# Reordering the on-chip tensors of an encoder layer so that the large ones begin at multiples of 2048 bytes

## The chip, the cores and the metric

The kernel runs on one core of a Trainium2 chip. The metric is the device time of one execution in microseconds, lower being better. The kernel before takes 1151.82 us, the median of 3 runs (1151.05 to 1152.61).

## The reference, cut to what matters

One layer of a streaming encoder on 256 tokens of width 2048, all in float32:

```python
h   = rms_norm(x, ln1);  p = h @ w_in            # 2048 x 5376
r   = retention(...)     # 8 heads of 128, rotary, group norm, swish gate
s   = sliding_window_attention(...)   # 16 query heads, 2 key/value heads, sinks
x   = x + concat([r, s]) @ w_out                 # 2048 x 2048
u   = rms_norm(x, ln2) @ w_ffn_in                # 2048 x 11264
a,b = split(u);  a = causal_depthwise_conv(a)    # width 3
x   = x + (gelu(a) * b) @ w_ffn_out              # 5632 x 2048
y   = rms_norm(x, ln_f)
```

The weights are about 200 MB and each is read once.

## The kernel before, in words

**Tiles.** Every weight is streamed from device memory in tiles of 128 rows (partitions) by 1024 float32 numbers, 4096 bytes in each partition. SyncE issues the loads into a ring of eight slots, `raw` (lines 313 to 320). ScalarE rounds a tile into `w_hi` (line 720), VectorE writes the difference `raw - w_hi` into `w_lo` (line 957); both are rings of four slots. TensorE multiplies in its one-pass float32 format (float32r) and so needs the activations split in the same way: `h_both` holds the high and low halves of the normalised input side by side, `mix_hi` and `mix_lo` those of the attention's output, `g_hi` and `g_lo` those of the gated hidden layer.

**Two forms of product.** In the input projection, the attention's output projection and the down projection (`three_pass`, lines 413 to 416) a block of activations of 128 columns is the stationary operand and 512 columns of `w_hi` or `w_lo` (256 in the first four tiles, which hold keys and values) are the moving one: `hi*hi`, `hi*lo`, `lo*hi`, three matmuls for each block. In the up projection (`up_tile`, lines 622 to 632) the weights are the stationary operand, four column blocks of 512 bytes each for each row block, and the activations are the moving one. One matmul takes all 512 numbers of a row block of `h_both` (line 630: high and low half at once), the next the 256 of the high half (line 632).

**Order.** The stages run one behind the other: keys and values, queries, eight heads with the attention of one head interleaved between the projection tiles of the next, the output projection, eleven groups of the up projection, the down projection in two sweeps, the last norm. All waits are written out by hand on semaphores: a load waits until its slot in `raw` has been read, ScalarE waits for the load and for the matmuls of the tile four before, VectorE for ScalarE, and TensorE for VectorE.

**Where tensors lie.** On-chip memory is given out in the order of the declarations, each tensor at the next address in the partition that is a multiple of 32 bytes. The first one declared begins at byte 16512 of the partition, which is 8 x 2048 + 128. Declared are first `x_res` (16384 bytes), `raw` (32768), `w_hi` and `w_lo` (16384 each), all of them multiples of 2048 bytes long, so that all four begin 128 bytes past a multiple of 2048. Then come the small ones: `ident` (512 bytes), `cols` (896), `sumsq` (32) and six tensors of 8 bytes, each of which takes 32. The tensors of the first part follow, `h_both`, `mix_hi`, `mix_lo`, `rows` and `rope` at 1760 bytes past a multiple of 2048; behind `mask` (1280 bytes) they lie at various remainders. The second part takes the same space again, with `y_tok`, `lnf_row`, `under_h`, `g_tok`, `g_hi`, `g_lo`, `sums` and `conv`, all of them at remainder 1760.

The slices that the matmuls read are multiples of 512 bytes from the start of these tensors. A moving operand of 512 columns of `w_hi` so begins at remainder 128, one of `h_both` at 1760. In the key and value tiles a row block of weights is 1024 bytes wide and begins at remainder 128 or at 1152, by turns; one that begins at 1152 ends at 2176 and runs over a multiple of 2048, one that begins at 128 does not.

Of the kernel before, what the change touches and what calls it, by code (L numbers as in the profile page):

```python
# [23 lines left out]
F32R = mybir.dt.float32r  # L24
# [6 lines left out]
P = 128  # L31
D_MODEL = 2048
SEQ = 256
TOK = SEQ // P
KT = D_MODEL // P
COLS = 512
# [24 lines left out]
RAW = 8  # L61
SPLIT = 4
# [42 lines left out]
def build(nc, x, ln1, w_in, b_swa, ret_gn, sinks, w_out, ln2, w_ffn_in, conv_w, conv_b, w_ffn_out,  # L105
# [10 lines left out]
    with ExitStack() as ctx:  # L116
        def sb(name, shape, dt=F32, scope=ctx):
            return scope.enter_context(nc.sbuf_tensor(name, shape, dt))
# [2 lines left out]
            return ctx.enter_context(nc.semaphore(name))  # L121


        x_res = sb("x_res", [P, TOK, D_MODEL])
        raw = sb("raw", [P, RAW, 2 * COLS])
        w_hi = sb("w_hi", [P, SPLIT, 2 * COLS], F32R)
        w_lo = sb("w_lo", [P, SPLIT, 2 * COLS], F32R)
        ident = sb("ident", [P, P])
        cols = sb("cols", [P, N_COLS])
        sumsq = sb("sumsq", [P, TOK, BLOCKS])  # L130
# [1 line left out]
        meansq = sb("meansq", [P, TOK])  # L132
        rstd = sb("rstd", [P, TOK])
        root_y, root_h, root_t = (sb(f"root_{c}", [P, TOK]) for c in "yht")


        part1 = ctx.enter_context(ExitStack())
# [1297 lines left out]
```

## Time and profile before

| what | value |
|---|---|
| median of the runs | 1151.82 us |
| the profiled execution's own time | 1153.21 us |
| its span, first to last instruction | 1151.4 us |
| TensorE matmul busy | 1133.4 us, 98% |
| VectorE busy | 699.5 us, 61% |
| ScalarE busy | 552.9 us, 48% |
| GpSimd busy | 76.1 us, 7% |
| loads and stores | 206.8 MB, 180 GB/s |
| mean granted TensorE clock | 0.995 of full |

Matmuls are pipelined: each takes longer from start to end than the distance to the next one's start, so that the busy time overlaps itself. The time that a matmul costs in a stream is the distance between two starts, and is read from the timeline. The clock is granted in two levels, 1.2 and 2.4 GHz; 1.00 is the upper one.

### The profile page before, as it was taken

What the parts mean: (1) busy time and instruction counts of PE and PEld (TensorE: products, weight loads), DVE (VectorE), ACT (ScalarE), POOL (GpSimd) and SP (SyncE); (2) the same over time, 40 slices, a digit from 0 to 9 for tenths busy, and PEclk for the clock granted to TensorE, in tenths of its full rate; (3) what the DMA queues carried; (4) which work ended last, traced back from release to release, by engine and by line L of the source; (5) the groups of instructions that cost most, each with busy time, mean ns of one, the idle gap of its engine ahead of it and who ended that gap; (6) DMA issues with size and microseconds to landing.
All of it is one profiled execution on the core that took longest, in us unless ns stands there. A gap on an engine that the chain in (4) does not pass through costs nothing.

```text
span 1151.4 us, 16731 instructions
## 1 busy us (share of the span) xinstructions
PE 1133.4 (98%) x5730; PEld 949.3 (82%) x5730; DVE 699.5 (61%) x1010; ACT 552.9 (48%) x760; POOL 76.1 (7%) x87
## 2 busy tenths in 40 slices
PE   8999999999999999999999999999998999999996
PEld 6888888888888888888888888888887888888885
DVE  5655666666656575656666656657556555575555
ACT  5434444444435445544544545445445444454443
POOL 2000111111100001101101101001011000000000
PEclk9999999999999999999999999999999999999999
DMA  9765555554555666666666666666665555555541
GB/s 326 251 183 166 150 151 151 149 146 146 149 170 175 183 182 184 185 193 187 184 188 192 183 186 190 189 183 187 193 184 188 182 189 188 183 184 191 189 130 73
DMA packets 146240, 206.80 MB, mean 180 GB/s; under 512 B 7539, under 2 KB 75537, under 8 KB 145952
## 3 DMA queue, kind: packets, MB, share of 16 engines
q1 hardware_dynamic: 145632, 204.67, 59.0%
q0 software_dynamic: 544, 1.72, 0.4%
q8 instruction: 18, 0.29, 0.1%
q14 instruction: 14, 0.11, 0.0%
q10 hardware_dynamic: 32, 0.01, 0.0%
HBM read 204.17 MB, written 2.10 MB: 179 GB/s over the span
## 4 chain that ended last, share of the span: by engine, by line
PE 96%; DMA 1%; DVE 1%; ACT 0%; SPq 0%; issue 0%; DVEq 0%; ACTq 0%
PE acc L630 14%; PE acc L414 13%; PE acc L415 13%; PE acc L416 13%; PE acc L632 7%; PE bank_s L630 7%; PE bank_tr L630 7%; PE bank_tr L632 4%; PE bank_s L632 4%; PE bank_s L416 2%; PE bank_s L414 2%; PE bank_s L415 2%; PE bank_tr L416 2%; PE bank_tr L414 2%; PE bank_tr L415 2%; DMA raw<-in_w_in 1%
## 5 line engine op out<-in xcount | busy, mean ns | idle before, releaser
L957 DVE TENSOR_TENSOR w_lo<-raw,w_hi 128x1024 fp32r<-128x1024 f32 x380 | 465.7, 1226 | 418.4 <-ACT w_hi L720 416.2
L720 ACT ACTIVATE w_hi<-raw 128x1024 fp32r<-128x1024 f32 x380 | 402.7, 1060 | 581.4 <-PE acc L416 196.4
L630 PE MATMUL acc<-h_both,w_hi 128*128 128x512 f32 x704 | 254.4, 394 | 0.0
L632 PE MATMUL acc<-h_both,w_lo 128*128 128x256 f32 x704 | 196.7, 279 | 0.0
L630 PEld LDWEIGHTS acc<-h_both,w_hi 128*128 128x128 f32 x704 | 132.0, 188 | 31.4
L414 PE MATMUL acc<-w_hi,h_both 128*128 128x512 f32 (+1 forms) x352 | 142.0, 404 | 0.2
L415 PE MATMUL acc<-w_lo,h_both 128*128 128x512 f32 (+1 forms) x352 | 136.2, 387 | 0.0
L416 PE MATMUL acc<-w_hi,h_both 128*128 128x512 f32 (+1 forms) x352 | 136.1, 387 | 0.0
L632 PEld LDWEIGHTS acc<-h_both,w_lo 128*128 128x128 f32 x704 | 132.1, 188 | 0.0
L630 PE MATMUL bank_tr<-h_both,w_hi 128*128 128x512 f32 x352 | 127.0, 393 | 0.0
L630 PE MATMUL bank_s<-h_both,w_hi 128*128 128x512 f32 x352 | 127.0, 393 | 0.0
L632 PE MATMUL bank_s<-h_both,w_lo 128*128 128x256 f32 x352 | 98.3, 279 | 0.0
L632 PE MATMUL bank_tr<-h_both,w_lo 128*128 128x256 f32 x352 | 98.3, 279 | 0.0
L630 PEld LDWEIGHTS bank_tr<-h_both,w_hi 128*128 128x128 f32 x352 | 66.0, 187 | 15.8
L630 PEld LDWEIGHTS bank_s<-h_both,w_hi 128*128 128x128 f32 x352 | 66.0, 187 | 15.8
L414 PEld LDWEIGHTS acc<-w_hi,h_both 128*128 128x128 f32 x352 | 66.9, 190 | 14.7 <-DVE h_both L964 0.8
L416 PEld LDWEIGHTS acc<-w_hi,h_both 128*128 128x128 f32 x352 | 66.8, 190 | 14.5
L415 PEld LDWEIGHTS acc<-w_lo,h_both 128*128 128x128 f32 x352 | 67.0, 190 | 13.5
L414 PE MATMUL acc<-w_hi,g_hi 128*128 128x512 f32 x176 | 70.6, 401 | 3.2 <-DVE g_lo L1246 3.2
L415 PE MATMUL acc<-w_lo,g_hi 128*128 128x512 f32 x176 | 70.5, 401 | 0.0
L416 PE MATMUL acc<-w_hi,g_lo 128*128 128x512 f32 x176 | 70.3, 400 | 0.0
L1383 POOL TENSOR_TENSOR conv<-conv,rstd_row 128x512 f32<-128x512 f32 x22 | 33.7, 1532 | 531.7 <-ACT conv L863 531.7
(171 smaller groups left out, 1396.8 us busy)
## 6 DMA issues: line engine op xcount, KB each, us to landing
raw<-in_w_ffn_in SPq DMA_DIRECT2D x176, 512.0 KB, 3.6
raw<-in_w_ffn_out SPq DMA_DIRECT2D x88, 512.0 KB, 4.6
raw<-in_w_in SPq DMA_DIRECT2D x128, 256.0 KB, 3.1
raw<-in_w_out SPq DMA_DIRECT2D x32, 512.0 KB, 4.0
raw<-in_w_in SPq DMA_DIRECT2D x20, 512.0 KB, 9.4
x_res<-in_x SPq DMA_DIRECT2D x4, 512.0 KB, 10.3
decay<-table_decay POOLq DMA_DIRECT2D x1, 1024.0 KB, 9.7
lnf_row<-in_ln_f SPq DMA_DIRECT2D x1, 1024.0 KB, 6.8
```

The costliest lines, as they stand in the source:

```text
L414: mm(out, lhs_hi, rhs_hi, start=first, stop=False, skip_group_check=True)
L415: mm(out, lhs_hi, rhs_lo, start=False, stop=False, skip_group_check=True)
L416: return mm(out, lhs_lo, rhs_hi, start=False, stop=last, skip_group_check=True)
L630: mm(out, w_hi[:, slot, w], h_both[:, 2 * k + q, :, :].rearrange("p a n -> p (a n)"), start=k == 0 and q == 0, stop=False, skip_group_chec ...
L632: ins = mm(out[:, 0:SEQ], w_lo[:, slot, w], h_hi[:, 2 * k + q, :], start=False, stop=k == 7 and q == 1, skip_group_check=True)
L720: run(w_hi[:, n % SPLIT, :], raw[:, n % RAW, :], ACT.Copy).then_inc(hi_ready, 1)
L957: tt(w_lo[:, n % SPLIT, :], raw[:, n % RAW, :], w_hi[:, n % SPLIT, :].bitcast(F32), ALU.subtract).then_inc(lo_ready, 1)
L1383: nc.gpsimd.tensor_tensor(conv[:, own, :], conv[:, own, :], rstd_row[:].unsqueeze(1).broadcast_to([P, 2, SEQ]), ALU.mult).then_inc(gate_re ...
```

## The change

The four large tensors are declared behind the small ones, and a tensor of 288 bytes that nothing reads or writes, `to_2048`, is declared ahead of them.

```diff
-        x_res = sb("x_res", [P, TOK, D_MODEL])
-        raw = sb("raw", [P, RAW, 2 * COLS])
-        w_hi = sb("w_hi", [P, SPLIT, 2 * COLS], F32R)
-        w_lo = sb("w_lo", [P, SPLIT, 2 * COLS], F32R)
         ident = sb("ident", [P, P])
         cols = sb("cols", [P, N_COLS])
         sumsq = sb("sumsq", [P, TOK, BLOCKS])
...
         root_y, root_h, root_t = (sb(f"root_{c}", [P, TOK]) for c in "yht")
+        to_2048 = sb("to_2048", [P, 72])
+        x_res = sb("x_res", [P, TOK, D_MODEL])
+        raw = sb("raw", [P, RAW, 2 * COLS])
+        w_hi = sb("w_hi", [P, SPLIT, 2 * COLS], F32R)
+        w_lo = sb("w_lo", [P, SPLIT, 2 * COLS], F32R)
```

The small tensors now take bytes 16512 to 18143, the filler 18144 to 18431, and `x_res` begins at 18432, which is 9 x 2048. `raw`, `w_hi` and `w_lo` follow at remainder 0, and so do `h_both` and what was at remainder 1760 with it. Tensors declared from `decay` on lie 288 bytes further on than before. The last tensor ends at 229040 of 229344 usable bytes. No instruction, no wait, no size and no order of work is changed.

## Rows read from the trace of the kernel before

**Rows 1.** The page: busy times, then the chain that ended last by engine.

```profile
PE 1133.4 (98%) x5730; PEld 949.3 (82%) x5730; DVE 699.5 (61%) x1010; ACT 552.9 (48%) x760; POOL 76.1 (7%) x87
...
PE 96%; DMA 1%; DVE 1%; ACT 0%; SPq 0%; issue 0%; DVEq 0%; ACTq 0%
```

**Rows 2.** Waits over the whole span: total us, times, longest.

```profile
ACT w_hi L720 <- PE acc L416: 196.4, 103, 3.7
...
ACT w_hi L720 <- DMA raw<-in_w_in: 11.1, 4, 5.0
...
PE acc L414 <- DVE g_lo L1246: 3.2, 1, 3.2
```

**Rows 3.** Instructions by line and shape: count, then busy us and mean ns.

```profile
L957 DVE TENSOR_TENSOR w_lo<-raw,w_hi 128x1024 fp32r<-128x1024 f32 x380 | 465.7, 1226 | 418.4 <-ACT w_hi L720 416.2
...
L630 PE MATMUL acc<-h_both,w_hi 128*128 128x512 f32 x704 | 254.4, 394 | 0.0
...
L414 PE MATMUL acc<-w_hi,h_both 128*128 128x512 f32 x320 | 132.3, 413 | 0.0
...
L1246 DVE TENSOR_TENSOR g_lo<-g_tok,g_hi 128x512 fp32r<-128x512 f32 x44 | 30.1, 685 | 0.0
```

**Rows 4.** Timeline of TensorE in the up projection: start us, length us.

```profile
500.24 0.39 PE L630 MATMUL bank_s<-h_both,w_hi 128*128 128x512 f32 x1
500.47 0.28 PE L632 MATMUL bank_s<-h_both,w_lo 128*128 128x256 f32 x1
500.59 0.39 PE L630 MATMUL bank_s<-h_both,w_hi 128*128 128x512 f32 x1
...
500.94 0.39 PE L630 MATMUL bank_s<-h_both,w_hi 128*128 128x512 f32 x1
...
501.29 0.40 PE L630 MATMUL bank_s<-h_both,w_hi 128*128 128x512 f32 x1
...
508.64 0.39 PE L630 MATMUL bank_tr<-h_both,w_hi 128*128 128x512 f32 x1
```

**Rows 5.** Timeline of TensorE in the down projection.

```profile
1000.35 0.40 PE L414 MATMUL bank_s<-w_hi,g_hi 128*128 128x512 f32 x1
...
1007.38 0.40 PE L414 MATMUL bank_s<-w_hi,g_hi 128*128 128x512 f32 x1
```

**Rows 6.** Timeline, last key and value tile: line 414 of four row blocks.

```profile
25.59 0.28 PE L414 MATMUL acc<-w_hi,h_both 128*128 128x256 f32 x1
...
25.94 0.28 PE L414 MATMUL acc<-w_hi,h_both 128*128 128x256 f32 x1
...
26.30 0.28 PE L414 MATMUL acc<-w_hi,h_both 128*128 128x256 f32 x1
...
26.65 0.28 PE L414 MATMUL acc<-w_hi,h_both 128*128 128x256 f32 x1
```

**Rows 7.** Timeline, start of the down projection.

```profile
891.36 0.77 PE L414 MATMUL acc<-w_hi,g_hi 128*128 128x512 f32 x1 [3.16 <-DVE g_lo L1246]
...
892.35 0.63 PE L416 MATMUL acc<-w_hi,g_lo 128*128 128x512 f32 x1
...
897.04 0.62 PE L415 MATMUL acc<-w_lo,g_hi 128*128 128x512 f32 x1
```

**Rows 8.** Windows: length, busy us by engine, clock, DMA share, GB/s.

```profile
0.00:30.00 30.00, 24.81 (x149) 20.46 (x150) 14.44 (x26) 17.64 (x28) 7.12 (x16) 1.00 0.96 329
...
500.00:600.00 100.00, 100.00 (x574) 87.28 (x573) 61.39 (x70) 48.62 (x63) 6.13 (x4) 1.00 0.65 188
...
1130.00:1152.00 22.00, 11.79 (x51) 9.15 (x49) 12.03 (x38) 5.88 (x11) 2.85 (x1) 0.88 0.24 95
```

**Rows 9.** The chain that ended last, 4 to 22 us: start, length.

```profile
4.08 14.22 DMA raw<-in_w_in
...
18.32 1.07 ACT w_hi L720
...
19.41 1.23 DVE w_lo L957
20.64 1.58 DVE h_both L964 x4
```

**Rows 10.** DMA issues: count, KB each, median us from issue to landing.

```profile
raw<-in_w_ffn_in SPq DMA_DIRECT2D x176, 512.0 KB, 3.6
raw<-in_w_ffn_out SPq DMA_DIRECT2D x88, 512.0 KB, 4.6
```

## The prediction

> **What bounds the kernel now.** I read the page first. TensorE has a matmul under way in 98% of the span, and 96% of the chain that ended last is TensorE; DMA has 1% [rows 1]. Then the waits: ScalarE, the first engine behind the loads, waits for matmuls again and again (one of several such groups is shown) and for a load only four times, 11.1 us together; TensorE's longest wait is one of 3.2 us [rows 2]. So in the steady stretches the loads are ahead of ScalarE, and ScalarE and VectorE ahead of TensorE. In 500 to 600 us the DMA engines are busy 0.65 of the time and VectorE 61 us of 100 [rows 8]. The time is the number of matmuls times the distance between their starts, and a start and an end around it.
>
> **The distances.** An address can act on the time through these above all. In the up projection 24 pairs start between 500.24 and 508.64, so a pair takes 350.0 ns: 512 and 256 columns, 0.456 ns a column [rows 4]. In the down projection 30 matmuls of 512 columns start between 1000.35 and 1007.38: 234.3 ns each, 0.458 ns a column [rows 5]. At 2.4 GHz one column a cycle would be 0.417, so about 9% is lost. At 1.2 GHz nothing is: 11 starts between 892.35 and 897.04 give 426.4 ns each, and 512 / 1.2 is 426.7 [rows 7]. The loss is there only at the upper clock and grows with the columns, which looks like a limit on how fast the moving operand can be read, and not like a fixed cost of each matmul. This is what a change of addresses could touch, and it is large. There are 1408 pairs (704 + 352 + 352) and 2400 three-pass matmuls of 512 columns (3 x 800, of which 320 stand in [rows 3]). Against one column a cycle (320.0 ns a pair, 213.3 ns a matmul) they lose 1408 x 30.0 ns = 42.2 us and 2400 x 21.0 ns = 50.4 us: 92.6 us.
>
> **The change, part by part.**
>
> *The instructions.* None is added, removed or moved; nothing touches the filler. No queue is passed and no wait is new: 0 us.
>
> *The moving operand.* Each 512-column read now begins 128 or 1760 bytes past a multiple of 2048 and runs over one such multiple; after the change each begins on one and runs over none. Two rows say what that is worth. First, 128 is a multiple of 128, and 1760 only of 32; if the start mattered at a grain between the two, the two forms of product would differ. They do by 0.002 ns a column, and the less aligned one is the faster [rows 4, 5]. Second, in the last key and value tile the second row block (from 25.59) and the fourth (from 26.30) run over a multiple of 2048 and the third (from 25.94) does not. Their three matmuls take 0.35, 0.35 and 0.36 us [rows 6]. A crossing thus costs less than the 0.01 us that three matmuls resolve, some 3 ns a matmul, and what is seen has the wrong sign. I take 0. The bounds: if the three-pass matmuls came down to the rate of the up projection, 512 x 0.4557 = 233.3 ns, they would give 2400 x 1.0 ns = 2.4 us. If it is the up projection that goes to the other's rate, 768 x 0.4577 = 351.5 ns a pair, it costs 1408 x 1.5 ns = 2.1 us, and if the three-pass matmuls lose another 1.0 ns each, 2.4 us more. So -2.4 to +4.5 us, and I take the middle that the rows say, nothing. No row shows a start at remainder 0, which is why a chance is kept for more.
>
> *The stationary operand.* The blocks of `w_hi` begin at 128, 640, 1152 and 1664, so their places against the moving operand at 1760 already differ by four amounts, and the last one crosses a multiple of 2048. A pair of the third block, at 500.24, and one of the fourth, at 500.94, both take 0.35 us, as the mean of 24 pairs over all four blocks does [rows 4]. 0 us.
>
> *VectorE and ScalarE.* VectorE's subtraction takes 1226 ns for 1024 elements whose three operands all begin at remainder 128, and 685 ns for 512 whose operands begin at 1760 [rows 3]. That is 541 ns for 512 more elements, and 144 ns fixed in both if the remainder does nothing; two sizes alone can't exclude that it does something. `raw`, `w_hi` and `w_lo` keep their distances from each other. But the work is covered: VectorE is idle for 418.4 us just ahead of its subtractions, nearly all of it in waits for ScalarE [rows 3]. Uncovered it is at the end, where some 12 us of VectorE and 6 us of ScalarE lie in the last 22 us [rows 8]; 1% of that would be 0.2 us. 0 us.
>
> *The loads.* `raw` goes from remainder 128 to 0. A load of the up projection lands 3.6 us after its issue and one of the down projection 4.6 us [rows 10], into a ring of eight tiles, where TensorE takes 8 pairs, 2.8 us, for a tile [rows 4]; a faster load ends earlier in a slot that waits. It counts at the start alone: the chain runs through 14.22 us of a load, then ScalarE, VectorE and the turned input block, and only then through matmuls [rows 9]. At 329 GB/s and a DMA share of 0.96 that stretch is bound by the engines' rate [rows 8]. Bounds: all four waits gone, -11.1 us [rows 2]; a tenth slower or faster, 1.4 us either way; I take 0, since all destinations of these loads have the same remainder now and no row shows another.
>
> The Trainium skill, in "DMA: Bandwidth & Descriptors", section "How a descriptor splits into AXI transactions", says that a transaction has to start at a 256-byte boundary and that bytes ahead of an unaligned start still cost beats. If that holds for the written side too, a piece of 2048 bytes at remainder 128 takes nine transactions in place of eight; an estimate from this page is 14.22 / 9 = 1.6 us less at the start. No row here has an aligned piece to set beside it.
>
> *The clock.* It falls to the lower level once inside the kernel, behind the wait of 3.16 us at the start of the down projection, a wait for a chain of ScalarE and VectorE work that no address changes [rows 7]. Neither the wait nor the fall should move.
>
> **The sum** is 0 against the profiled execution's own 1153.21 us (span 1151.4 and 1.8 around it). That execution lies 0.12% above the median of the runs; so I forecast the median, 1151.8 us. A measurement of this kernel tells about 0.2%, 2.3 us, from no change.
>
> **The rivals.**
>
> *The loads at the start become faster.* For it: the stretch is bound by DMA and on the chain [rows 8, 9]. Against: nothing shows that the remainder matters. By a ninth of 14.22 us it gives 1.6 us: 1150.2, which counts as no change. It decides only from a gain of 2.3 us, a sixth of the load. It is the skill's rule above turned into a time; chance 0.08.
>
> *The three-pass matmuls reach the up projection's rate.* For it: the small difference between [rows 4] and [rows 5] needs some cause, and remainder 128 may be it. Against: 1760 is the worse remainder by any power of two. It gives -2.4 us, 1149.4; with some gain of the loads, clearly faster. Chance 0.08.
>
> *The reading limit goes altogether.* The 9% come from reads that are not at remainder 0, and vanish: 92.6 us, 1059. For it: the loss is proportional to columns and so one of reading [rows 4, 5, 7]. Against: two unlike starts lose the same, and a read without a crossing does too [rows 6]. Chance 0.02. The skill's page "TensorE: Matmul & The Clock Gate", section "Back-to-back issue gap", gives N / 2.4 + 2.5 ns, 215.8 ns for 512 columns. The trace disagrees with 234.3 ns, and if the alignment were what makes the difference, the estimate from the page would be 1408 x 25.0 + 2400 x 18.5 ns = 79.6 us less.
>
> *Everything at the same remainder collides: slower.* After the change the moving operand, the stationary one, and what ScalarE and VectorE read and write all begin at remainder 0. If the memory is divided by low address bits, streams that start together stay together and stall each other. It decides from 0.6 ns for each of the 1408 pairs and 2400 three-pass matmuls (2.3 us / 3808). Price by the bounds above, 1.5 ns a pair and 1.0 ns a three-pass matmul: +4.5 us, 1156.3. Against: one block of `w_hi` in four already begins 96 bytes from the moving operand's remainder (1664 and 1760) and its pairs keep the mean [rows 4]. Chance 0.06.
>
> **How the numbers follow.** No effect: 0.76, at 1151.8; the rivals have 0.08, 0.08, 0.02 and 0.06. Faster: 0.08 + 0.02, and 0.01 of the case of the loads, 0.11. Slower: 0.06, and 0.01 of the case of no effect for what I haven't thought of, 0.07. What is left of those two, 0.75 + 0.07, is within 0.2%: 0.82. The range that holds 8 in 10 is the no-change case with the measurement's 2.3 us, stretched down to take in the rate case: 1149.2 to 1154.3.
>
> **What would show it right or wrong.** The distance of pairs should be 350 ns and that of three-pass matmuls 234 ns, both to 1 ns; if the limit is one of addresses, these two move first and everywhere alike. The row of the chain that begins near 4 us would be shorter than 14.22 us if the loads gained. VectorE's 1226 ns and ScalarE's rounding should stay. There should be one fall of the clock, near 891 us. I am wrong if the distance of the matmuls depends on the remainder at 0 in a way that neither 128 nor 1760 lets one see.

## The result, and the profile after

The changed kernel takes 1142.14 us, the median of 4 runs (1140.14 to 1143.62), against 1151.71 us before (4 runs): a ratio of 0.9914, 95% interval 0.9902 to 0.9927. It is 9.6 us faster, where I forecast no change and a range from 1149.2. The profiled execution has a span of 1139.5 us, 11.9 less than before. All ratios here are of fast executions: two slow ones of the later comparisons, 2876.31 us of the kernel with weights at 128 and activations at 0 and 2262.59 us of the kernel before, are left out of them.

The page of the changed kernel, its first line and the busy times. Lines of the code have moved by one.

```profile
span 1139.5 us, 16731 instructions
...
PE 1122.0 (98%) x5730; PEld 948.9 (83%) x5730; DVE 699.2 (61%) x1010; ACT 552.9 (49%) x760; POOL 76.1 (7%) x87
```

The same number of instructions; VectorE and ScalarE are busy as long as before and TensorE 11.4 us less [rows 1]. So it is TensorE's own rate. The waits of the changed kernel say the same, beside those of before [rows 2]: ScalarE still waits for matmuls, for a load only three times (9.8 us together), and TensorE's longest wait is again 3.2 us.

```profile
ACT w_hi L721 <- PE acc L417: 189.0, 103, 3.6
```

The timeline of TensorE in the up projection, for [rows 4], 24 pairs apart:

```profile
499.85 0.40 PE L631 MATMUL acc<-h_both,w_hi 128*128 128x512 f32 x1
...
508.33 0.40 PE L631 MATMUL acc<-h_both,w_hi 128*128 128x512 f32 x1
```

A pair now takes 8.48 / 24 = 353.3 ns, where it took 350.0: slower. In the down projection, for [rows 5], 30 matmuls apart:

```profile
999.62 0.39 PE L415 MATMUL bank_s<-w_hi,g_hi 128*128 128x512 f32 x1
...
1006.42 0.39 PE L415 MATMUL bank_s<-w_hi,g_hi 128*128 128x512 f32 x1
```

That is 6.80 / 30 = 226.7 ns, where it was 234.3: faster by 7.6. Two things of opposite sign have happened, and both in TensorE's stream. Read by stage, from the starts of the first and last matmul of each in the two timelines:

| stage | before | after | difference |
|---|---|---|---|
| start, to the first 512-column matmul of the queries | 28.07 us | 27.16 us | -0.91 |
| queries, heads, output projection (1344 three-pass matmuls of 512 columns) | 365.92 | 358.17 | -7.75 |
| up projection (1408 pairs) | 493.93 | 498.48 | +4.55 |
| wait at the start of the down projection | 3.44 | 3.44 | 0 |
| down projection (1056 three-pass matmuls) | 250.03 | 242.03 | -8.00 |
| end | 10.03 | 10.24 | +0.21 |

1056 x 7.6 ns is 8.0 us, and 1408 x 3.3 ns is 4.6 us: the distances account for the last two stages of matmuls. In the first, 1344 x 7.6 ns would be 10.2 us and it gained 7.75. By the starts in the two traces, 1233 of its distances went from a mean of 234.1 to 228.0 ns: in the changed kernel the first few behind each interruption still take up to 237 ns, and only then come the 226.7. The other 110 distances, which hold other matmuls or a wait, stay at 77 us in all.

### The profile page after: what moved, and what is told of

Same layout as the page of the kernel before. It is cut to its first block, busy times and chain, and to the rows that moved or that the text cites. A ratio compares the mean times of both kernels' runs of the same rounds, so it can differ in the third digit from the quotient of the medians.

```text
span 1139.5 us, 16731 instructions
## 1 busy us (share of the span) xinstructions
PE 1122.0 (98%) x5730; PEld 948.9 (83%) x5730; DVE 699.2 (61%) x1010; ACT 552.9 (49%) x760; POOL 76.1 (7%) x87
## 4 chain that ended last, share of the span: by engine, by line
PE 97%; DMA 1%; DVE 1%; ACT 0%; SPq 0%; issue 0%; DVEq 0%; ACTq 0%
PE acc L631 15%; PE acc L415 13%; PE acc L417 13%; PE acc L416 13%; PE acc L633 7%; PE bank_s L631 7%; PE bank_tr L631 7%; PE bank_tr L633 4%; PE bank_s L633 4%; PE bank_s L416 2%; PE bank_s L415 2%; PE bank_s L417 2%; PE bank_tr L415 2%; PE bank_tr L416 2%; PE bank_tr L417 2%; DMA x_res<-in_x 1%
## 5 line engine op out<-in xcount | busy, mean ns | idle before, releaser
L958 DVE TENSOR_TENSOR w_lo<-raw,w_hi 128x1024 fp32r<-128x1024 f32 x380 | 465.5, 1225 | 407.6 <-ACT w_hi L721 405.8
L415 PE MATMUL acc<-w_hi,h_both 128*128 128x512 f32 (+1 forms) x352 | 140.4, 399 | 0.2 <-DVE h_both L965 0.2
L417 PE MATMUL acc<-w_hi,h_both 128*128 128x512 f32 (+1 forms) x352 | 134.4, 382 | 0.0
```

The source lines that it names most:

```text
L415: mm(out, lhs_hi, rhs_hi, start=first, stop=False, skip_group_check=True)
L417: return mm(out, lhs_lo, rhs_hi, start=False, stop=last, skip_group_check=True)
L958: tt(w_lo[:, n % SPLIT, :], raw[:, n % RAW, :], w_hi[:, n % SPLIT, :].bitcast(F32), ALU.subtract).then_inc(lo_ready, 1)
```

## Experiments

**Which operand: the two groups apart.** One kernel has the weight rings at remainder 0 and the activations at 1760, the other the weights at 128 and the activations at 0.

```diff
 # weights 0, activations 1760: small tensors and filler of 288 bytes ahead of x_res, and behind w_lo
+        mask = sb("mask", [P, P + KEYS1])
+        neg_sink = sb("neg_sink", [P, SWA_HEADS])
...
+        r_denom = sb("r_denom", [P, 4])
+        pad_1077 = sb("pad_1077", [P, 8])
 # weights 128, activations 0: the kernel before, and behind root_t
+        pad_512 = sb("pad_512", [P, 72])
```

> Weight rings w_hi and w_lo at remainder 0 as in the changed kernel, activations (h_both, mix, g_hi, g_lo) at 1760 as before. Theory A, the moving operand's own start sets the distance of matmuls: three-pass matmuls (moving w) 227 ns as in the changed kernel, pairs of the up projection (moving h_both) 350 ns as before, so about 1151.4 - 17.5 = 1134 us. Theory B, the stationary operand's start sets it: three-pass 234 ns, pairs 353.3 ns, about 1156 us. Theory C, both must be at one remainder (their difference counts): three-pass between, pairs not 350, some 1142 to 1152 us.

> The mirror: weights at remainder 128 as before, activations at 0 as in the changed kernel. Theory A (moving operand's start): three-pass 234 ns, pairs 353.3 ns, about 1151.4 + 4.7 = 1156 us. Theory B (stationary operand's start): three-pass 227 ns, pairs 350 ns, about 1134 us. Theory C (difference): neither value of before nor of after in at least one form.

The first took 1154.94 us against 1152.58 before (ratio 1.0008, interval 0.9984 to 1.0032), span 1153.7; the second 1150.63 us (0.9989, 0.9977 to 1.0001), span 1148.4. Neither has the gain. One of the first kernel's ten executions, however, took 1142.90 us and the others 1153.28 to 1156.59; it is in the ratio and has no trace. The timelines, first of weights 0 and activations 1760, then of weights 128 and activations 0; in each, 24 pairs of the up projection and then 30 three-pass matmuls of the down projection:

```profile
499.51 0.40 PE L632 MATMUL bank_s<-h_both,w_hi 128*128 128x512 f32 x1
...
507.99 0.40 PE L632 MATMUL bank_s<-h_both,w_hi 128*128 128x512 f32 x1
...
999.65 0.40 PE L416 MATMUL acc<-w_hi,g_hi 128*128 128x512 f32 x1
...
1006.65 0.40 PE L416 MATMUL acc<-w_hi,g_hi 128*128 128x512 f32 x1
```

```profile
499.55 0.40 PE L631 MATMUL bank_s<-h_both,w_hi 128*128 128x512 f32 x1
...
507.98 0.40 PE L631 MATMUL bank_tr<-h_both,w_hi 128*128 128x512 f32 x1
...
999.60 0.41 PE L417 MATMUL acc<-w_hi,g_lo 128*128 128x512 f32 x1
...
1006.58 0.39 PE L417 MATMUL acc<-w_hi,g_lo 128*128 128x512 f32 x1
```

Pairs take 353.3 and 351.3 ns, three-pass matmuls 233.3 and 232.7. Theory A is out by the first kernel, where it had 227 and 350. Theory B named the first kernel's distances (234 and 353.3) and is out by the second, where it had 227 and 350. Among these four kernels the three-pass 226.7 ns stands only where both groups are at 0, and each has another three-pass distance, as theory C has it. Its time of 1142 to 1152 us for the first kernel was missed by 3 us.

**Streams of matmuls alone.** Four kernels, two of them here and two further down, leave the layer out and run forms of the product back to back, on slices of two large tensors at chosen remainders, with no other engine at work.

```python
def three_pass(acc, w, h):           # w, h: bytes past a multiple of 2048
    ...
    for n, (moving, own) in enumerate(((w0, h0), (w0 + 4096, h0), (w0, h0 + SEQ))):
        mm(acc[:, t, :], big_h[:, own:own + P], big_w[:, moving:moving + 512], ...)
def up(acc, w, h):
    ...
    mm(acc[:, ft, :], big_w[:, w0:w0 + P], big_h[:, h0:h0 + 512], ...)
    mm(acc[:, ft, 0:SEQ], big_w[:, w0 + 4096:w0 + 4096 + P], big_h[:, h0:h0 + SEQ], ...)
```

> Only streams of matmuls on one core, in the two forms of the kernel, with operands from two large tensors at chosen remainders; the layer is left out and the output is x. Names: t or u for three-pass or up form, w and h for bytes past a multiple of 2048. If addresses alone make the difference, t at w128 h1760 takes 234 ns, t at w0 h0 227 ns, u pairs at w128 h1760 350 ns and at w0 h0 353 ns, with no other engine at work. Theory A: t changes along w only, u along h only. Theory B: the other way round. Theory C: both change with w - h. If the kernel's other engines or absolute places are needed, all segments of a form take the same.

> Streams of matmuls alone (the layer is left out, the output is x), every difference of the two operands' starts from 0 to 224 bytes in steps of 32, the other being a multiple of 2048; each of the up form with 0, 1 and 2 short matmuls ahead, each of the three-pass form with 0 and 1; order shuffled. Theory D, the difference modulo 256 sets the distance: three-pass 226.7 ns at difference 0 and 229 to 234 ns at all others, whatever stands ahead. Rival, the history sets it (a stream falls into one of several rhythms as it begins): the same difference takes different times behind different heads. For the up form I expect 353.3 ns at most differences and 346.7 at some; if the history counts, both values at one difference.

The first kernel repeats what the whole kernels do. The means of the distances in a segment of 72 matmuls or 48 pairs, its first few left out, were 226.7 ns at (0, 0) and 233.3 at (0, 1760) and (128, 0) for three-pass (weights, activations); for pairs 350.0 at (128, 1760), 353.1 at (0, 1760), 351.0 at (128, 0). In the first segment, at (128, 1760), the median is 234, since its first matmuls ran at the lower clock. So addresses alone do it, and no other engine is needed. Three-pass at (256, 0), (512, 0), (1024, 0), (1792, 0), (0, 256), (0, 512), (0, 1024), and also at (32, 32), (128, 128) and (1024, 1024), takes 226.7 to 226.8 ns. A multiple of 2048 isn't needed: what counts is the difference of the two starts, modulo 256. The up form took 346.7 ns a pair at (0, 0), but 353.1 at the ten other places of the same kernel with a difference of 0, the first sign of what comes below. The second kernel measured all differences in steps of 32 bytes, in mixed order (means over some 40 to 70 distances, of which those of pairs are good to some 0.4 ns):

| weights minus activations, modulo 256 | 0 | 32 | 64 | 96 | 128 | 160 | 192 | 224 |
|---|---|---|---|---|---|---|---|---|
| three-pass, ns a matmul | 226.7 | 233.3 | 228.9 | 233.3 | 232.5 | 234.3 | 233.3 | 233.3 |
| up, ns a pair | 346.7 or 353.5 | 353.3 | 353.3 | 346.7 | 351.2 | 350.0 | 348.9 or 353.2 | 346.7 |
| the whole kernels there | after | weights 0, acts 1760 | | | weights 128, acts 0 | before | | |

The kernel before is at 128 - 1760 = 160 modulo 256, and the two mixed ones are at 32 and 128: each has the distances of its column. Three-pass at 128 isn't quite one value: both segments of the second kernel take 232.5 ns, and 233.3 was measured in the first and in a later one, at the same addresses. The two segments of the up form at difference 0, in the timeline of this second kernel (line 71, 24 pairs each, behind two short matmuls and behind one):

```profile
202.95 0.40 PE L71 MATMUL _w_zero_h_zero_ahead_two<-big_h,big_w 128*128 128x512 f32 x1
...
211.43 0.40 PE L71 MATMUL _w_zero_h_zero_ahead_two<-big_h,big_w 128*128 128x512 f32 x1
...
219.64 0.39 PE L71 MATMUL _w_zero_h_zero_ahead_one<-big_h,big_w 128*128 128x512 f32 x1
...
227.96 0.39 PE L71 MATMUL _w_zero_h_zero_ahead_one<-big_h,big_w 128*128 128x512 f32 x1
```

8.48 / 24 = 353.3 ns in the one, 8.32 / 24 = 346.7 in the other, with the same operands at the same addresses. At this difference, and for pairs at 192, the rival is right too: the stream has two rhythms and keeps the one that it fell into. At 224 (activations 32 bytes further) and at 96 (activations 160 bytes further) all three tries gave 346.7.

**The difference in the whole kernel, and a better one.** Three kernels ran side by side. One is the kernel before with a filler of 416 bytes behind the small tensors, so that both groups lie at remainder 128. One is the changed kernel with the second norm's output, which the up projection reads, 32 bytes further than the first norm's. The third is the changed kernel again.

```diff
 # both at 128: the kernel before, and behind root_t
+        pad_512 = sb("pad_512", [P, 104])
 # activations of the up projection 32 bytes further: the changed kernel, and
-        h_both = s1("h_both", [P, KT, 2, SEQ], F32R)
+        h_room = s1("h_room", [P, KT * 2 * SEQ + 64], F32R)
+        h_both = h_room[:, 0:KT * 2 * SEQ].rearrange("p (t a n) -> p t a n", t=KT, a=2)
+        h_up = h_room[:, 8:KT * 2 * SEQ + 8].rearrange("p (t a n) -> p t a n", t=KT, a=2)
...
-        under_h = sb("under_h", [P, D_MODEL])
+        under_h = sb("under_h", [P, D_MODEL + 64])
...
-                        mm(out, w_hi[:, slot, w], h_both[:, 2 * k + q, :, :].rearrange("p a n -> p (a n)"),
+                        mm(out, w_hi[:, slot, w], h_up[:, 2 * k + q, :, :].rearrange("p a n -> p (a n)"),
...
```

> The kernel before with nothing but a filler of 416 bytes behind the small tensors, so that weights and activations both begin 128 bytes past a multiple of 2048 (loads go to remainder 128 as before). Theory D: difference 0, so the same as the changed kernel, three-pass 227 ns and pairs 353.3 ns, span about 1139.5 us. If the multiples of 2048 count: pairs 350, three-pass 234 ns, 1151.4 us. What is left between this one and the changed kernel is the remainder of the loads' destinations, at the start, by the rule on 256-byte boundaries 1.6 us.

> The changed kernel with one more shift: the normalised activations that the up projection reads lie 32 bytes further than those of the input projection (mix, g_hi and g_lo stay at multiples of 256, behind a filler). Theory D, the difference of the two operands' starts modulo 256 sets the distance: pairs at activations 32 bytes behind the weights take 346.7 ns as in the streams alone, where the changed kernel has 353.3; three-pass matmuls stay at 226.7 to 229 ns. 1408 x 6.6 ns = 9.3 us less: a span of 1130 us. If instead multiples of 2048 matter for themselves, pairs stay at 353 ns or get slower, and the span is 1139 us or more.

> The changed kernel again, beside the two: span about 1139.5 us, pairs 353.3 ns, three-pass 226.7 ns in the down projection.

Both at 128: 1140.84 us against 1151.81 before (0.988, interval 0.9829 to 0.993), span 1139.1, pairs 353.3 ns, and three-pass, again 30 matmuls apart:

```profile
999.63 0.39 PE L417 MATMUL bank_s<-w_hi,g_lo 128*128 128x512 f32 x1
...
1006.43 0.39 PE L417 MATMUL bank_s<-w_hi,g_lo 128*128 128x512 f32 x1
```

6.80 / 30 = 226.7 ns. A filler of 416 bytes alone does what the change does. Activations of the up projection 32 bytes further: 1131.45 us (0.9817, interval 0.98 to 0.9835), span 1130.0, as theory D had it. Its timeline:

```profile
499.69 0.39 PE L634 MATMUL acc<-h_room,w_hi 128*128 128x512 f32 x1
...
508.01 0.39 PE L634 MATMUL acc<-h_room,w_hi 128*128 128x512 f32 x1
```

346.7 ns a pair; a three-pass matmul takes 226.7, as in the changed kernel. The changed kernel again, however, was not what I had expected: 1134.23, 1140.71, 1140.61 and 1130.93 us. The profiled execution is the one of 1134.23, and its timeline of the up projection, again over 24 pairs, is:

```profile
499.78 0.39 PE L631 MATMUL acc<-h_both,w_hi 128*128 128x512 f32 x1
...
508.10 0.39 PE L631 MATMUL acc<-h_both,w_hi 128*128 128x512 f32 x1
```

8.32 / 24 = 346.7 ns. The same program had 353.3 in its first profile. Here are the two rhythms of difference 0 in the whole kernel; each lasts for the whole up projection (from 40 us behind its start on, every stretch of 20 us has the same mean to 0.4 ns), and the two are 1408 x 6.6 ns = 9.3 us apart; the stage took 498.5 us in the one and 489.5 in the other. The kernel with both groups at 128 shows the same spread: 1140.85, 1141.95, 1131.86 and 1140.84 us. Which rhythm the executions without a profile had I take from their times alone: of the 12 at difference 0, three lie between 1130.9 and 1134.3 us, the other nine between 1140.1 and 1143.7. The one execution of 1142.90 us with weights at 0 and activations at 1760 hints at a second rhythm there too, 10 us and more below the others; no trace shows it.

**Is it stable?**

> The same kernel as e3_up_acts_32, for the spread. If activations 32 bytes behind the weights leave the up projection one rhythm alone, all runs lie within some 3 us of 1131.5; if there are two rhythms here too, some lie 9 us higher.

> As e3_up_acts_32, with the up projection's activations 160 bytes further than the weights, the other difference at which the streams alone took 346.7 ns in all three tries. Theory D: 346.7 ns a pair and a span of 1130 us, in every run. Rival: only a small difference helps, 353 or 350 ns a pair, 1135 to 1140 us.

> Streams alone (the layer is left out, the output is x). The up form at difference 0 and at 32 bytes, each behind 0 to 7 short matmuls: if difference 0 has two rhythms, some of its eight segments take 346.7 ns a pair and others 353.3, while all eight at 32 bytes take 346.7. Three-pass form with 128 to 504 moving columns at differences 0 and 32: if each matmul costs its columns at 2.4 GHz and a fixed 13.3 ns at difference 0, then 120.0 ns for 256, 173.3 for 384, 200.0 for 448; if the loss is proportional to the columns, 113.3, 170.0 and 198.3.

These three ran on another chip than the experiments above. Again at 32 bytes: 1131.2 us, 5 runs from 1129.55 to 1132.87 (0.9826, interval 0.9808 to 0.9843). At 160 bytes: 1131.33 us, 4 runs from 1129.2 to 1132.31 (0.9823, interval 0.9804 to 0.9843), span 1129.1. None of the 13 runs at these two differences lies near 1140. In the streams alone all eight segments at 32 bytes take 346.7 ns a pair; at difference 0 all eight took 353.1 to 353.4. Over the three kernels of streams that makes the lower rhythm 3 of 22 segments at difference 0, and the number of short matmuls ahead doesn't choose it: behind one, a pair took 346.7 ns in one kernel and 353.2 in another. Here my expectation of a mixture failed.

The widths of the moving operand at difference 0, in the timeline of the same kernel (36 matmuls of 256 columns in a row; the last one's own length, 0.28 us, isn't a distance):

```profile
427.78 4.48 PE L108 MATMUL w_zero_h_zero_ahead_zero<-big_w,big_h 128*128 128x256 f32 x36
```

4.20 / 35 = 120.0 ns for 256 columns. With 146.7 for 320, 173.3 for 384 and 226.7 for 512 that is the columns at 2.4 GHz and 13.3 ns at each of the four widths; it isn't proportional. At other widths it isn't as smooth: 202.7 for 448 (2.7 ns over the rule), 216.7 for 480 (3.3 over), 226.7 for 504 (3.3 over), and 111.7 for both 192 and 128, where something else is the limit. At difference 32 the same widths take 116.7 (256), 173.3 (384) and 206.7 (448) ns: the difference that is best depends on the width.

**Is it the load of the stationary operand?**

> Streams of matmuls alone (the layer is left out, the output is x). If the lost time is that of two reads meeting, of the moving operand and of the next stationary one, it must shrink with the stationary operand's columns: three-pass at 64 and 32 stationary columns nearer to 213.3 ns than 226.7 and less sensitive to the difference. If it is a limit on reading the moving operand alone, 64 and 32 columns keep 226.7 ns at difference 0 and 233.3 at 32. Differences of 4, 8 and 16 bytes: if a line of memory is 32 bytes or longer, near 226.7 ns, otherwise 233.3. bfloat16 (half the bytes): 216 ns at every difference. 256 moving columns: 120 ns at difference 0 as in the kernel's first tiles.

It was inconclusive. Three-pass with 64 stationary columns takes 230.0 ns at difference 0 and 230.8 at 32; with 32 columns 231.6 and 226.7. Fewer columns neither bring the time near 213.3 nor keep the values of 128 columns; they change which difference is the best. So the stationary operand does take part, but no width of it comes below the 226.7 ns of 128 columns. Steps below 32 bytes matter as well: three-pass at 4, 8 and 16 bytes takes 237.6, 233.3 and 231.6 ns. bfloat16 takes 215.8 ns a matmul at differences 0, 32 and 128.

## Why the prediction was wrong

**What bounds the kernel** was right: TensorE's rate times its count of matmuls, and the distances were where the change showed. Noticing the loss above one column a cycle was right, too, and the two distances did move first, though not alike. The condition that I gave for being wrong came near: it named the remainder at 0, and with both groups at 128 the distances are the same as at 0. How the loss grows was read wrongly, as proportional to the columns. It is 13.3 ns for each matmul at difference 0, of 256 columns as of 512, and on top of it, before, 7.6 ns for a three-pass matmul and 3.3 for a pair.

**The step that failed** is "The moving operand", the term taken as nothing with bounds of -2.4 and +4.5 us. In its place the stages showed -15.8 us for the 2400 three-pass matmuls (5.8 ns each in the first 1344, 7.6 in the last 1056), and +4.6 us for 1408 pairs at 3.3 ns more. Its argument had three comparisons, and none of them had a case of difference 0; two of them held the difference fixed altogether. The remainder of one operand does nothing by itself; the difference of the two does, modulo 256. The two forms were compared at differences 160 and -160 (96) of the moving from the stationary operand, neither of them 0. The crossing test compared row blocks 1024 bytes apart. "The stationary operand" compared column blocks 512 bytes apart. Both steps are multiples of 256, so that the "four amounts" of the latter are all 96 modulo 256. That so many unlike addresses took the same time looked like evidence that addresses don't matter, and it was evidence only for steps of 512.

**The bounds** came from rows that had no case like the new one, which I wrote, and then gave too little: I gave 0.11 to all that is faster.

**The rivals.** "The three-pass matmuls reach the up projection's rate" had the right place and a price of -2.4 us where it measured -15.8, since it took the up projection's own rate as the floor. "Everything at the same remainder collides" had the wrong sign for three-pass matmuls. For pairs its sign held in this execution, at more than twice its price (4.6 us, where it had 2.1), and in another of the same program the up projection took 489.5 us, 4.4 less than before: luck, as far as it goes. "The reading limit goes altogether" didn't happen: 13.3 ns a matmul stay in the best kernel. The net gain of 9.6 us isn't a fixed worth of the change either: with the lower rhythm the same program took 1130.9 and 1134.2 us.

**The other steps** held. VectorE's subtraction takes 1225 ns after 1226 [rows 3], and ScalarE's busy time is the same. The clock falls once inside the kernel, behind a wait of 3.16 us as before [rows 7]:

```profile
887.25 0.76 PE L415 MATMUL acc<-w_hi,g_hi 128*128 128x512 f32 x1 [3.16 <-DVE g_lo L1247]
```

In both traces the lower clock then lasts 6.8 us, so the stages above compare like with like. It isn't always so: over the nine traces of whole kernels the gap ahead of the down projection is the same 3.44 us, and the lower clock behind it lasts 6.8 us in three, 3.4 in five and is absent in one. At 226.7 ns a matmul the down projection takes 242.0 us with 6.8 us of it, 240.6 to 240.9 with 3.4 and 239.2 without.

**The loads** gain nothing that can be seen. In the changed kernel the start is 0.91 us shorter, but over all profiles the first 512-column matmul starts at 27.16, 27.47, 28.35, 29.14, 29.15 and 29.40 us with loads at remainder 0, and at 28.07, 28.08 and 28.78 with loads at 128. The row of 14.22 us in the chain at the start isn't a sign either: the load in that chain took 12.03 us in the kernel with weights at 128 and activations at 0, where the loads lie as before. The Trainium skill's rule on 256-byte boundaries in "DMA: Bandwidth & Descriptors", section "How a descriptor splits into AXI transactions", would have given 1.6 us. The prediction got this estimate from nine transactions for eight in pieces of 2048 bytes; the key and value tiles at the start have pieces of 1024, for which the section's way of counting gives 36 beats in place of 32, and by that estimate the same 1.6 us. No run here shows such a gain.

## What to carry to other kernels

Where a float32r stream of matmuls bounds the kernel, measure the distance between starts and compare it with the columns at the granted clock; if it is more, try the difference of the two operands' addresses modulo 256, one form of product at a time. Before taking equal times at unlike addresses as evidence, work out which combination of the addresses the comparison leaves fixed. And run a changed layout several times: at some differences the same program has two rhythms.

## What the runs showed of the hardware

- A float32r matmul of 128 stationary and 512 moving columns takes 226.7 to 234.3 ns in a stream at 2.4 GHz, by the difference of its two operands' starts modulo 256 in steps of 32 bytes (237.6 at 4 bytes). The difference decides nearly all: at 128 there are two values, 232.5 and 233.3 ns. bfloat16 takes 215.8 ns at any of the three differences tried. At 1.2 GHz the kernel before takes 426.4 ns, so that nothing is lost there [rows 7].
- Most float32r means lie on a raster of 6.67 ns, which is 16 cycles at 2.4 GHz: 226.7 and 233.3 are 34 and 35 of them, 346.7 and 353.3 are 52 and 53, 120.0 and 173.3 are 18 and 26. The rates in between (228.9, 232.5, 234.3, 350.0) are means over distances that repeat in a longer pattern. The 116.7 ns of 256 columns at difference 32 are an exception, 17.5 of them with equal distances. What the 16 cycles are, no run here shows.
- The Trainium skill, "TensorE: Matmul & The Clock Gate", section "Step-by-step: what each phase is for", says that the moving operand and the weight load have two independent read ports, and that loading the next weights takes nothing from the running matmul. For float32r the runs don't go with this as it stands: the relation of the two addresses changes the rate by 3.4% (226.7 to 234.3 ns). That the two reads meet in the memory is my reading, and it wasn't shown; the runs with fewer stationary columns speak neither for it nor clearly against it.
- An up projection at difference 0 runs at 346.7 or 353.3 ns a pair for its whole length of some 490 us. What chooses the rhythm stays open.
